# Taking out 22 filling matmuls ahead of each up projection in a hybrid decoder layer

## The reference

```
h = rmsnorm(x, norm1_g) * (1 + sc1) + sh1
x = x + g1 * hybrid_mixer(h, ...)          # SSD scan and gMLP side by side, then w_out
h = rmsnorm(x, norm2_g) * (1 + sc2) + sh2
x = x + g2 * conv_gated_ffn(h, ff_up, ff_conv_w, ff_conv_b, ff_down)
return rmsnorm(x, final_g)
```

## Time and profile before

| | |
|---|---|
| time, median of 3 runs | 3033.74 us (3032.5 to 3036.54) |
| span of the profiled execution | 3029.5 us |
| median less the span | 4.2 us |
| TensorE busy | 2892.4 us, 95% of the span |
| VectorE, POOL, ScalarE busy | 61%, 45%, 36% |
| TensorE's mean granted clock | 0.997 |
| filling matmuls (L1170) | 88, in four groups of 22 |

### The profile page before, as it was taken

How to read it: one execution, slowest core, us unless ns; L and a number is a source line. 1 busy time by engine, 2 the same in 40 slices (tenths; PEclk the granted TensorE clock), 3 DMA queues, 4 the chain that set the end, 5 groups by cost and what they waited for, 6 DMA issues and landing times.

```text
span 3029.5 us, 42819 instructions
## 1 busy us (share of the span) xinstructions
PE 2892.4 (95%) x13303; PEld 2366.1 (78%) x13303; DVE 1846.2 (61%) x2844; ACT 1082.4 (36%) x1734; POOL 1377.8 (45%) x960
## 2 busy tenths in 40 slices
PE   1889999999999999999998999999999999999998
PEld 1568888888877888888887788888887788888886
DVE  4685846565377774565628685565546778365653
ACT  0343333343334333343324433343333443243432
POOL 0543444555444344555444334455554434455553
PEclk9999999999999999999999999999999999999999
DMA  8343222334243322333334232233434332233332
GB/s 314 108 129 112 80 91 80 100 93 142 91 141 101 112 77 77 101 92 101 132 116 140 84 101 86 82 93 100 132 98 127 126 101 77 87 87 100 93 136 101
DMA packets 201303, 329.04 MB, mean 109 GB/s; under 512 B 18389, under 2 KB 110009, under 8 KB 197051
## 3 DMA queue, kind: packets, MB, share of 16 engines
q1 hardware_dynamic: 197394, 324.09, 33.9%
q10 hardware_dynamic: 3754, 2.96, 0.3%
HBM read 318.46 MB, written 8.53 MB: 108 GB/s over the span
## 4 chain that ended last, share of the span: by engine, by line
PE 84%; issue 7%; DVE 5%; ACTq 1%; POOL 1%; DMA 1%; ACT 0%; DVEq 0%; POOLq 0%
PE main L981 73%; PE main L1008 2%; PE pair L1084 2%; DVE acc L699 1%; POOL w_lo L354 1%; PE pair L1069 1%; PE pair L934 1%; DVE arow L744 1%; PE pair L1109 1%; PE pair L1076 1%; ACTq L380 1%; DMA small<-in_ssd_dt_bias_dram 1%; PE pair L1022 0%; PE pair L1120 0%; PE pair L1131 0%
## 5 line engine op out<-in xcount | busy, mean ns | idle before, releaser
L354 POOL TENSOR_TENSOR w_lo<-w_raw,w_hi 128x512 fp32r<-128x512 f32 x944 | 1353.4, 1444 | 1551.8 <-ACT w_hi L396 1050.9
L396 ACT ACTIVATE w_hi<-w_raw 128x512 fp32r<-128x512 f32 x595 | 371.3, 630 | 1002.6 <-PE main L981 756.8
L981 PE MATMUL main<-h_hi,w_hi 128*128 128x512 f32 x1776 | 695.2, 391 | 12.8 <-POOL w_lo L354 12.3
L981 PE MATMUL main<-h_lo,w_hi 128*128 128x512 f32 x1776 | 691.4, 389 | 0.0
L981 PE MATMUL main<-h_hi,w_lo 128*128 128x512 f32 x1776 | 691.3, 389 | 0.0
L981 PEld LDWEIGHTS main<-h_hi,w_hi 128*128 128x128 f32 x1776 | 333.4, 188 | 90.1 <-POOL w_lo L354 19.1
L981 PEld LDWEIGHTS main<-h_hi,w_lo 128*128 128x128 f32 x1776 | 333.4, 188 | 69.6
L981 PEld LDWEIGHTS main<-h_lo,w_hi 128*128 128x128 f32 x1776 | 333.5, 188 | 68.1
L515 ACT ACTIVATE w_hi<-w_raw 128x512 fp32r<-128x512 f32 x352 | 216.8, 628 | 394.9 <-PE main L981 394.9
L981 PE MATMUL main<-w_hi,h_hi 128*128 128x512 f32 x768 | 319.0, 415 | 0.0
L981 PE MATMUL main<-w_hi,h_lo 128*128 128x512 f32 x768 | 300.3, 391 | 0.0
(11 more groups left out here) (199 smaller groups left out, 4081.9 us busy)
## 6 DMA issues: line engine op xcount, KB each, us to landing
w_raw<-in_ff_up_dram SPq DMA_DIRECT2D x352, 256.0 KB, 3.1
w_raw<-in_w_in_dram SPq DMA_DIRECT2D x292, 256.0 KB, 2.8
w_raw<-in_ff_down_dram SPq DMA_DIRECT2D x176, 256.0 KB, 2.7
w_raw<-in_w_out_dram SPq DMA_DIRECT2D x128, 256.0 KB, 2.6
ada_t<-in_ada_w_dram SPq DMA_DIRECT2D x24, 1024.0 KB, 13.6
arow<-acs_scratch SPq DMA_DIRECT2D x16, 1024.0 KB, 4.8
x<-in_x_dram SPq DMA_DIRECT2D x4, 2048.0 KB, 8.0
xn<-in_x_dram SPq DMA_DIRECT2D x16, 512.0 KB, 8.0
```

What stands on the lines that cost most here:

```text
L354: nc.gpsimd.tensor_tensor(w_lo[:, s, :], w_raw[:, s, :], w_hi[:, s, :].bitcast(F32), ALU.subtract).then_inc(w_lo_ok, 1)
L396: nc.scalar.activation(w_hi[:, n % RING, :], w_raw[:, n % RING, :], ACT.Copy).then_inc(w_hi_ok, 1)
L981: ins = T.matmul(main[i][:], a, w, start=first and p == 0, stop=last and p == 2)
```

## The change

The loop with the 22 matmuls is deleted. The waits behind it and everything else stay as they are, on all engines.

```
                 bank_by_bank(OUT + 2 * KD, 2 * KD, out_ops)
 
 
-                for i in range(22):
-                    T.matmul(aux[3], h_hi[:, 0, 0:P], h_hi[:, 0, :], start=True, stop=True)
                 pe.wait_ge(xn_ok, b * (NT + 2) + (NT + 1))
                 pe.wait_ge(xn_act_ok, b * 2 + 1)
                 xn2_tiles = [xn2[:, t, :] for t in range(NT)]
```

## The result

The changed kernel takes 3042.36 us (median of 7 runs, 3039.67 to 3044.52), the kernel before 3032.50 us beside it (7 runs, 3031.00 to 3036.54). The ratio is 1.0032, with a 95% interval of 1.0021 to 1.0042: slower by 6 to 13 us, with 9.9 us between the medians. A second set on another occasion gave 3041.56 against 3032.69 us, 8.9 us.

A forecast was written before the change was run, and what follows sets the result against it. TensorE's own work, waits and clock bound the kernel. Removing fillers gains 0, the low clock costs 4 x 2.1 = +8.5 us, on 3033.74 giving 3042.2 us; own range 3040 to 3044.5, 8 in 10 from 3036 to 3048.

The forecast's parts named there:

- The fillers stand beside the chain, so removing them gains nothing: After the output projection: 20.6 us of fillers run beside VectorE's and ScalarE's chain, so the gain is 4 x 0.
- The clock falls in all four blocks, and is already low at the restart: When the transposes behind L505 start: 6.6 us idle in place of 1.61 brings the granted clock to 0.50.
- The price, 2.12 us a block, between 0.8 and 3.4: Behind L505: 16 transposes and the first two up-projection matmuls at low clock, +8.5 us over four blocks.
- The transposes' own term: Behind L505: 16 transposes at low clock take 3.68 us against 1.96, 1.72 us more a block.
- The scan's falls are as easily one or three as two: Scan's first chunk, 2.81 us wait: low clock in two of four blocks, as easily one or three, 1.66 us each.
- 4.2 us between median and span: Whole kernel: the median exceeds the profiled span by 4.2 us, added to 3038.0 us to give 3042.2.
- the first: Rival, behind L505: low clock lasts over all 16 transposes and a stretch of matmuls; 3.4 us a block, 3047.2 us; chance 0.20.
- The second: Rival, wait before L505's transposes: low stretch ends within idle time, remainders cost 0 to 3.3 us; 3035.2 us; chance 0.19.
- The third: Rival, VectorE's last-bank add: fillers slow it, removal saves 0.35 us a block, 1.4 in all; 3032.3 us; chance 0.03 by itself.

The follow-up runs named there:

- e2: Kernel before with 28 filling matmuls in place of 22 ahead of the up projection: 3032.91 against 3032.68 us.
- e10: Kernel before with 36 filling matmuls in place of 22, overrunning the wait ahead of the up projection: 3040.13 against 3032.53 us.
- e7: Changed kernel with 11 filling matmuls added in the wait of the scan's first chunk: 3040.56 us against 3032.69 us for the kernel before.
- e3: Kernel before with 44 float32 transposes of 128x128 in place of the 22 filling matmuls: 3032.41 against 3032.68 us.
- e4: Kernel before, its 22 fillers kept, with 11 more filling matmuls in the wait of the scan's first chunk: 3029.66 against 3032.68 us.
- e6: Kernel before with 16 filling matmuls in place of 22 ahead of the up projection: 3041.99 against 3032.69 us.
- e5: Kernel before with the 22 fillers replaced by three behind a wait for VectorE's reciprocal roots: 3041.95 against 3032.69 us.

## Why the prediction was right

I had forecast +8.5 us on 3033.74, 3042.2 us. Measured were 3042.36 us, and +9.9 and +8.9 us in the two sets.

- *The fillers stand beside the chain, so removing them gains nothing.* Right: the wait is 6.94 us from start to start against 6.99. e2 and e10 show it from the other side: fillers are free up to the end of the wait and cost their full 1.41 us a block beyond it.
- *The clock falls in all four blocks, and is already low at the restart.* Right in both profiles. The fall lies 2.3 to 4.0 us ahead of it.
- *The price, 2.12 us a block, between 0.8 and 3.4.* Right in its parts (slow transposes, then slow matmuls), somewhat too high where the scan falls too (7.0 and 6.2 us in all, 1.75 and 1.55 a block) and right where it does not (e7, 8.6 us, 2.14 a block). The transposes' own term was as worked out in blocks 0 and 3 (3.67 against 3.68 us taken from the earlier trace rows) and a little less in the others; the number of matmuls at low clock behind them was 0 to 3. I had counted on 4.4 us of low clock at work in each block, and it was 3.8, 3.1, 2.9 and 4.6 us.
- *The scan's falls are as easily one or three as two.* Right for the kernel before and its like (1 or 2 of 4), wrong for the changed one. They went to 4 of 4, in both of its profiles, and cost some 3 us more. I took them for scatter that the change leaves alone, and put this term at nothing. This omission and the price that was too high nearly cancel: 6.2 to 7.0 us at the restart and 3.0 to 4.4 in the scan, in place of 8.5. That the sum came so close to +8.9 and +9.9 us is in part luck.
- *4.2 us between median and span.* Wrong as a reading: it is 1.75 us, and the profiled execution of before was simply a faster one than the median (3029.5 + 1.75 = 3031.3 us). The difference that I forecast does not depend on it. The absolute time came out within 0.2 us by luck: I started from 3033.74 us, which is 1.2 us above the median of 7 runs, and my difference was 1.4 us too small.

Of the rivals, the first (the transposes do not bring the clock back, +13.5) fell with e3 and with block 1 of the profile after. The second (the low stretch ends inside the wait) did not happen: in both profiles of the changed kernel all low stretches at the restart lasted 6.8 us, and so outlasted the wait. The 3.4 us of the earlier trace rows were no fixed length. The third (the fillers slow VectorE) is refuted by the add for the last bank, which takes as good as the same without them, against the 1.04 us of the earlier trace rows:

```profile
469.48 1.01 DVE L847 TENSOR_TENSOR x<-x,stage 128x512 f32<-128x512 f32 x1
```

## What to carry to other kernels

Matmuls that nobody reads can be worth their place: where TensorE is the bound and has to wait for some microseconds in each round of a loop, look at the granted clock behind the wait, and fill the wait almost to its end. Here 1.6 to 1.8 us left empty did no harm and 2.97 us lost everything; part of the filling was worth nothing, and what overran the wait cost in full. Look for every other wait of that size too (filling one of 2.81 us was worth 3.0 us in the kernel before, and only 1.0 us in the changed one). When a change alters the length of a loop's round by a microsecond or two, count the low stretches everywhere in the profile and not only at the edit.

## What the hardware did that I had not expected

- Idle times of 1.61 to 1.77 us never brought the clock down (0 of 12, at the restart in before, e3 and e4), one of 2.97 us did in all four blocks (e6), and one of 2.81 us did in anything from 1 to 4 blocks of 4, depending on the kernel around it.
- A fall at the restart or just behind it costs about as much as one well ahead of it: the time at work with a low clock sums to 12.6 us over e6's four blocks, against 14.4 and 12.9 us in the two profiles of the changed kernel, and 13.6 us with three late fillers (e5).
- The first block starts between 116.0 and 119.9 us in the profiles, by the length of one low stretch that begins at 103 to 106 us: 116.0 to 116.6 us with 3.4 us of low clock there, 117.5 to 117.8 with 6.8, 119.4 to 119.9 with 10.2. This scatter of some 4 us, which no kernel here changes on purpose, is more than e4's whole gain.
